# Opening pass over two tiles, outer decay levels as 32- and 64-blocks, and moved remainders at the last steps

## The reference, cut to what matters

```
x = x + 0.5 * swiglu(rmsnorm(x), w_gate, w_up, w_down)        # the opening
...
diff = bcum[..., :, None, :] - bcum[..., None, :, :]
decay = jnp.exp(jnp.where(tri, diff, -jnp.inf))
attn = jnp.einsum('zbhtk,zbhtsk->zbhts', qc, decay * kc[..., None, :, :])
...
x = x + (gelu(conv(h @ w_gate)) * (h @ w_up)) @ w_down        # the last step
gate = sigmoid(rmsnorm_2(x, norm_ple_g) @ w_ple_gate)
x = x + (p @ w_ple) * gate
return rmsnorm_2(x, final_norm_g)                             # the end
```

## Time and profile before

| | |
|---|---|
| median of 3 runs | 901.1 us (900.48 to 901.19) |
| the profiled execution | 901.16 us, its span 899.4 us |
| PE, DVE, ACT, POOL busy | 98%, 65%, 53%, 11% of the span |
| DVE remainder of a unit, L1841 / L1848 | 1259 / 1224 ns |
| ACT rounding of a unit, L1288 / L1297 | 1055 / 1058 ns |
| POOL x_lo of a chunk, L2711 | 1375 ns |
| HBM read | 155.56 MB, 174 GB/s over the span |

### The profile page before, as it was taken

The page is one execution under the profiler, slowest core; times in us unless marked ns, Lnnn a source line. Parts: engine busy times, 40 slices in busy tenths (PEclk is TensorE's granted clock), DMA queues, the critical chain, the costliest instruction groups (busy, mean ns, idle before and its releaser), DMA issues.

```text
span 899.4 us, 14824 instructions
## 1 busy us (share of the span) xinstructions
PE 877.5 (98%) x5181; PEld 733.5 (82%) x5181; DVE 587.2 (65%) x906; ACT 480.5 (53%) x727; POOL 97.3 (11%) x97
## 2 busy tenths in 40 slices
PE   6999999999999999999999999999999999999996
PEld 5788888878777778888888878878888999999875
DVE  5655555556689876655555567888776667667665
ACT  6544444447466746444444466666746445445464
POOL 6120000001000011000000022762011000000020
PEclk9999999999999999999999999999999999999998
DMA  9796666545654354755555537352246655655511
GB/s 313 228 269 197 204 212 193 174 154 165 203 175 138 95 164 140 230 191 187 186 188 186 189 105 245 119 179 101 91 147 211 206 183 179 193 186 181 190 51 47
DMA packets 122026, 157.23 MB, mean 175 GB/s; under 512 B 10047, under 2 KB 83011, under 8 KB 121984
## 3 DMA queue, kind: packets, MB, share of 16 engines
q1 hardware_dynamic: 119648, 151.65, 52.2%
q0 software_dynamic: 1888, 4.42, 2.0%
q10 hardware_dynamic: 448, 0.59, 0.2%
HBM read 155.56 MB, written 1.07 MB: 174 GB/s over the span
## 4 chain that ended last, share of the span: by engine, by line
PE 90%; DVE 5%; ACT 3%; issue 1%; DMA 1%; SPq 0%; DVEq 0%; ACTq 0%
PE bank L507 23%; PE bank L509 23%; PE bank L508 23%; PE bank L540 4%; PE bank L539 4%; PE bank L538 4%; PE bank L621 1%; DVE w_lo L1841 1%; PE bank L776 1%; PE bank L988 1%; PE bank L964 1%; DMA w_raw<-in_w_ffn_up 1%; PE bank L976 1%; ACT w_hi L1288 1%; DVE w_lo L1848 1%
## 5 line engine op out<-in xcount | busy, mean ns | idle before, releaser
L1848 DVE TENSOR_TENSOR w_lo<-w_raw,w_hi 128x1024 fp32r<-128x1024 f32 x180 | 220.2, 1224 | 176.0 <-ACT w_hi L1297 176.0
L1297 ACT ACTIVATE w_hi<-w_raw 128x1024 fp32r<-128x1024 f32 x180 | 190.3, 1058 | 207.0 <-PE bank L509 172.3
L507 PE MATMUL bank<-w_hi,x_hi 128*128 128x512 f32 (+1 forms) x688 | 276.4, 402 | 5.0 <-DVE w_lo L1841 1.8
L509 PE MATMUL bank<-w_hi,x_lo 128*128 128x512 f32 (+1 forms) x688 | 268.3, 390 | 0.0
L508 PE MATMUL bank<-w_lo,x_hi 128*128 128x512 f32 (+1 forms) x688 | 267.5, 389 | 0.0
L507 PEld LDWEIGHTS bank<-w_hi,x_hi 128*128 128x128 f32 x688 | 129.9, 189 | 35.6 <-issue 8.5
L509 PEld LDWEIGHTS bank<-w_hi,x_lo 128*128 128x128 f32 x688 | 129.7, 189 | 27.7
L1841 DVE TENSOR_TENSOR w_lo<-w_raw,w_hi 128x1024 fp32r<-128x1024 f32 x98 | 121.4, 1259 | 43.4 <-ACT w_hi L1288 43.2
L508 PEld LDWEIGHTS bank<-w_lo,x_hi 128*128 128x128 f32 x688 | 130.2, 189 | 23.9
L1288 ACT ACTIVATE w_hi<-w_raw 128x1024 fp32r<-128x1024 f32 x100 | 103.4, 1055 | 41.1 <-PE bank L509 33.6
L507 PE MATMUL bank<-w_hi,h_hi 128*128 128x512 f32 x272 | 107.6, 395 | 1.1 <-DVE h_lo L1958 0.5
(11 more groups left out here) (299 smaller groups left out, 815.0 us busy)
## 6 DMA issues: line engine op xcount, KB each, us to landing
w_raw<-in_w_ffn_gate SPq DMA_DIRECT2D x132, 256.0 KB, 2.9
w_raw<-in_w_ffn_up SPq DMA_DIRECT2D x132, 256.0 KB, 3.1
w_raw<-in_w_ffn_down SPq DMA_DIRECT2D x132, 256.0 KB, 3.0
w_raw<-in_w_in SPq DMA_DIRECT2D x104, 256.0 KB, 3.0
w_raw<-in_w_out SPq DMA_DIRECT2D x32, 256.0 KB, 3.4
w_raw<-in_w_ple_gate SPq DMA_DIRECT2D x16, 256.0 KB, 3.3
arena<-bias_rows POOLq DMA_DIRECT2D x8, 256.0 KB, 4.4
w_raw<-in_cmp_w_k SPq DMA_DIRECT2D x8, 256.0 KB, 3.7
```

The source lines that it names most:

```text
L507: pe.matmul(out_, hi, wh, start=start, stop=False)
L509: return pe.matmul(out_, lo, wh, start=False, stop=stop)
L1297: act.activation(whi[:, slot * UNIT:(slot + 1) * UNIT], raw[:, slot * UNIT:(slot + 1) * UNIT], ACT.Copy).then_inc(sem("hi_done"), 1)
L1848: dve.tensor_tensor(wlo[:, s_], raw[:, s_], whi[:, s_].bitcast(F32), ALU.subtract).then_inc(sem("lo_done"), 1)
```

## The change

- Opening, SP: x chunk 0, then the weight units 0 and 1, then x chunks 1 and 3, then the rest. ACT loads chunk 2 and four of the row loads, POOL the other seven.
- Opening, PE: nine matmuls on zeros before the first transposes, seven after the first two chunks, which are now 0 and 2 (`X_ORDER`), one of each tile. `opening()` takes the place of `tile_passes`: unit 0 over tile 0 and 1, unit 1 over both, then units 2 and 3 over tile 0, units 2 and 3 over tile 1, with the transposes of the third and fourth chunk behind the first and third of these products.
- Opening, ACT and DVE: squares of x before the rounding of unit 2, the root before that of unit 4; unit 5 after the silu of tile 0.
- Levels 6 and 7: blocks of h x h, 32 and 64, four and two for each 128 rows, each in its own strip; DVE's masked copy becomes two, one for each head of the pair, with the block's columns read repeatedly.
- Last step: convolution weights before the two scaled halves, the remainder of the second embedding unit behind the product of the convolution, that of gate unit 1 behind the second update of x, of gate unit 2 behind the fourth.
- End: the gain is multiplied ahead for chunks 0, 1 and 2; DVE multiplies the factor for chunk 0 and ACT for chunks 1 and 2; chunk 3 stays as it was. ACT stores chunk 2.

```diff
 def tile_passes / opening (PE)
+            def opening():
+                for m, j in ((0, 0), (1, 0), (0, 1), (1, 1), (0, 2), (0, 3), (1, 2), (1, 3)):
+                    if j % 2 == 0:
+                        pe.wait_ge(sem("xlo_done"), 2 * (j // 2) + m + 1)
+                    if m == 0:
+                        pe.wait_ge(*lo_ready(j + 1))
...
+                    if (m, j) == (0, 0):
+                        norm_chunk(0, 2)
+                    if (m, j) == (0, 1):
+                        norm_chunk(0, 3)
...
+            zeros = sg[:, 0:256].bitcast(BF16)
+            def warm(n):
+                for _ in range(n):
+                    pe.matmul(bank[0][:, :], zeros[:, 0:P], zeros[:, 0:512], start=True, stop=True)
+            pe.wait_ge(sem("warm_in"), 1)
+            warm(9)
...
-            for c in range(4):
+            for c in range(2):
                 norm_chunk(0, c)
+            warm(7)
             ffn(0, U_FFN1)
...
 level (PE)
-                        if 1 <= L <= 7:
-                            h, c = 1 << (L - 1), (2 * hh + blk) * P
-                            mm = pe.matmul(b[:, c:c + P], av(KMIX[pr] + hh * S + blk * P, [P]), both_ways(HQ + at, P, h),
-                                           start=True, stop=True)
+                        if L <= 7:
+                            h = 1 << (L - 1)
+                            c = (2 * hh + blk) * h
+                            for j in range(P // h):
+                                other = j ^ 1
+                                mm = pe.matmul(b[j * h:(j + 1) * h, c:c + h],
+                                               av(KMIX[pr] + hh * S + blk * P + j * h, [h]),
+                                               av(HQ + at + other * h + 1024 * (other % 2), [h]), start=True, stop=True)
...
 opening (ACT)
-            norm_hi(0, (0, 1))
+            act.dma_start(x_chunk(2), x_rows(2)).then_inc(sem("x_in2"), 16)
+            for to, r0, nr, src in row_loads[:4]:
+                act.dma_start(to[r0:r0 + nr, :], src).then_inc(sem("rows_act"), 16)
+            norm_hi(0, (0,))
             split(0)
+            norm_hi(0, (1,))
+            split(1)
...
+                squares(0, x, (m,))
+            split(2)
             norm_hi(0, (2,))
-            split(1)
+            split(3)
             norm_hi(0, (3,))
-            for v in range(2, RING):
-                split(v)
-            stats(0, x)
+            roots(0)
+            split(4)
...
 last step (DVE)
+                    if isinstance(i, int) and i > 1:
+                        conv_weights(STEPS)
+                        scaled_halves(i)
+                        return
...
-                conv_weights(STEPS)
                 conv_taps(STEPS)
...
                 conv_mul(STEPS)
+                split_step(base, STEPS - 1, 3)
...
                 split_step(base, STEPS - 1, 4)
-                split_step(base, STEPS - 1, 5)
...
-            split(U_GATE + 2)
             update = add_ffn(2, U_FFN3, 1.0)
             update(0)
             update(1)
             scaled(5, R_PLE, 0)
+            split(U_GATE + 1)
...
 end (DVE, ACT)
+            last_gain(0)
+            last_gain(2)
             gated(1, 0)
             last_mean(0)
+            last_gain(1)
             gated(1, 1)
-            dve.wait_ge(sem("gain_in"), 32)
-            last_scale(0)
+            dve.wait_ge(sem("rstd_done"), 8)
+            dve.wait_ge(sem("last_gain"), 1)
+            dve.tensor_scalar(x_chunk(0), x_chunk(0), sm(RST8), None, ALU.mult).then_inc(sem("out_ready"), 1)
             last_mean(1)
-            last_scale(1)
+            dve.wait_ge(sem("rstd_done"), 9)
+            dve.scalar_tensor_tensor(x_chunk(3), x_chunk(3), sm(RST8 + 1), gainb[:, 512:1024],
+                                     ALU.mult, ALU.mult).then_inc(sem("out_ready"), 1)
...
+            act.activation(x_chunk(1), x_chunk(1), ACT.Copy, scale=sm(RST8)).then_inc(sem("out_act"), 1)
             last_root(1)
+            act.wait_ge(sem("rstd_done"), 9)
+            act.activation(x_chunk(2), x_chunk(2), ACT.Copy, scale=sm(RST8 + 1)).then_inc(sem("out_act"), 1)
+            act.wait_ge(sem("out_act"), 2)
+            act.dma_start(out[0, P:2 * P, 0:512], x_chunk(2)).then_inc(sem("stored"), 16)
```

More of the change, by code:

```diff
@@ L428, in ffn @@
                     load_gu((base + j) % RING, wg, wu, j, slice(0, HID))
+                    if first and j == 1:
+                        x_load(1)
+                        x_load(3)
                 if first:
@@ L460, in blockload @@
                     load_cols((u + j) % RING, w, 2 * j, c0, width)
-            for c in range(2):
-                sp.dma_start(x_chunk(c), x_rows(c)).then_inc(sem(f"x_in{c}"), 16)
+            x_load(0)
             ffn(U_FFN1, t["w_ffn1_gate"][0], t["w_ffn1_up"][0], t["w_ffn1_down"][0], first=True)
@@ L622, in turn @@
                 mm.then_inc(sem("t_full"), 1)
+            def opening():
[4 more added lines that the diff above has]
+                        pe.wait_ge(*lo_ready(j + 1))
+                    wh = whi[:, j * UNIT:(j + 1) * UNIT].rearrange("p (k n) -> p k n", k=2)
+                    wl = wlo[:, j * UNIT:(j + 1) * UNIT].rearrange("p (k n) -> p k n", k=2)
+                    for kk in range(2):
+                        k = 2 * j + kk
+                        last = three(bank[m][:, :], xT(xhi, k, m), xT(xlo, k, m), wh[:, kk, :], wl[:, kk, :],
+                                     k == 0, k == 7)
+                    if m == 1:
+                        last.then_inc(sem("w_used"), 1)
+                    elif j == 3:
+                        last.then_inc(sem("tile0_full"), 1)
+                    if (m, j) == (0, 0):
+                        norm_chunk(0, 2)
+                    if (m, j) == (0, 1):
+                        norm_chunk(0, 3)
             def ffn(f, base):
@@ L671, in ffn @@
                     pe.wait_ge(sem("h_done"), 2 * n0)
-                tile_passes(base, (0, 1), ready=(0, 8)[f], nrm=(None, 2)[f])
                 if f == 0:
+                    opening()
                     columns()
+                else:
+                    tile_passes(base, (0, 1), ready=8, nrm=2)
                 gate_up_first(bias_rows if f == 0 else None)
@@ L1863, in norm_x, with means @@
                 scaled(n, gain, 3)
-            def rstd(n):
+            def means(n):
                 dve.wait_ge(sem("ss_done"), 2 * n + 2)
@@ L1870, in rstd @@
                 dve.reciprocal(sm(MS, 2), sm(MS, 2)).then_inc(sem("ms_done"), 1)
+            def rstd(n):
+                means(n)
                 dve.wait_ge(sem("rstd_done"), n + 1)
@@ L1897, in ffn @@
                 halves(0, (0,))
+                if f == 0:
+                    split(5)
                 split(base + RING)
@@ L1968, in step @@
                     split_step(base, i, 2)
+                    if isinstance(i, int) and i > 1:
+                        conv_weights(STEPS)
+                        scaled_halves(i)
+                        return
                     scaled_halves(i)
-                    for j in range(3, 4 if isinstance(i, int) and i > 1 else 6):
+                    for j in range(3, 6):
                         split_step(base, i, j)
@@ L2026, in _ @@
             dve.wait_ge(sem("gain0_done"), 1)
-            for c in range(3):
+            for c in range(2):
                 scaled(0, R_GAIN, c)
             split(0)
+            split(1)
+            scaled(0, R_GAIN, 2)
+            means(0)
+            split(2)
             scaled(0, R_GAIN, 3)
-            for v in range(1, RING):
-                split(v)
+            split(3)
+            split(4)
             def columns():
@@ L2664, in _ @@
             scaled(5, R_PLE, 2)
-            split(U_GATE + 3)
+            split(U_GATE + 2)
             scaled(5, R_PLE, 3)
-            for j in (4, 5):
+            for j in (3, 4, 5):
                 split(U_GATE + j)
```

62 lines of the change are left out of this document (39 added, 23 removed).

## The result

| | before | after |
|---|---|---|
| median of 5 runs each | 901.19 us (900.48 to 901.72) | 896.26 us (895.74 to 896.60) |
| ratio, 95% interval | | 0.9947 [0.9936, 0.9958] |
| profiled execution | 901.16, span 899.4 | 895.74, span 893.9 |
| PE busy | 877.5 | 877.1 |

A forecast was written before the change was run, and what follows sets the result against it. PE was taken to bound the kernel, busy 877.5 of 899.4 us. Opening 2.2, levels 0.4, last step 2.0 and end 0.9 sum to 5.5 us: 901.16 - 5.5 = 895.7 us, range 893.3 to 898.6.

The forecast's parts named there:

- First matmul at 10.0: Opening: with two transfers of 256 KB less ahead, the first f32r matmul starts 1.3 us earlier, bounds 0.5 and 2.0.
- The clock held: Opening: dummies keep PE at 2.4 GHz from the first matmul, saving 2.4 us, less 1.0 for transposes inside the pass.
- rival A: Opening: dummies do not hold the clock up, so it gives 0 to 0.9 us; total taken as 897.5; chance 0.20.
- End of the pass at 22.1, bias row at 28.8: Opening: pass ends 2.7 us earlier, but DVE's remainders and column copies hold the bias-row matmul until 28.8.
- Opening: 2.2 forecast: The whole opening was to give 2.2 us, bounds 0 (low clock) and 3.3.
- Levels 0.4: Levels 6 and 7: PE alone wins 1.7 us, 0.4 arrives, the rest becomes PE waiting for DVE; bounds -0.3 and 1.7.
- rival C: Level 7: 64-blocks don't run side by side and take 3.4 us instead of 1.7; total 896.9; chance 0.07.
- Rival B: Opening and levels: DVE does not pace them, giving 2.7 instead of 2.2 and 1.7 instead of 0.4; 893.9; chance 0.14.
- Last step 2.0: Third feed-forward block's last step: two PE gaps, 0.90 and 1.08 us, are covered; gain 2.0 us, bounds 1.0 and 2.1.
- The cover of 0.4 us for h_lo: Last step: the moved remainder stands ahead of h_lo, ready about 856.5 and needed at 856.95, leaving 0.4 us.
- End 0.9: After the last matmul: scaling split between DVE and ScalarE ends 1.3 us earlier; gain 0.9 us, bounds 0.3 and 1.3.
- that of the stores: End: the last two stores start together and share the rings, which costs 0.3 to 0.4 us.

The follow-up runs named there:

- the first set: The first five runs of the changed kernel, measured against the kernel before: 896.26 us against 901.19.
- level-7: The changed kernel with level 7 as one 128-wide matmul and one whole-bank copy, level 6 staying in 32-wide blocks: 895.55 us (0.9941).
- turn experiments: The changed kernel with column copies earlier, the turn of head 0 between the last unit's two tiles, ScalarE's scores ahead of its rounding: 895.20 us (0.9939).
- the second: Five more runs of the unchanged changed kernel, on one chip with three reordered kernels: 896.59 us (0.9954 to the kernel before).
- the old order: The kernel before with only the nine and seven dummy matmuls added, its order of the pass kept: 900.75 us (0.9995).

## Why the prediction was right, point by point

**First matmul at 10.0.** It was 10.34 in the first profiled execution and 9.48 to 10.60 over the seven: 0.94 us earlier where 1.3 was credited, and the clock less the transposes gave 1.61 where 1.4 was. The size of the gain from fewer transfers ahead was right within the spread of when transfers land, a spread for which the forecast had no term.

**The clock held: half right.** The spacing of 0.23 us from the start was seen in five of seven executions. In two rival A happened, for a cause that the forecast didn't name. It set rival A against the length of the dummies; the level fell behind the longest of the pauses that a late x chunk leaves between them (1.64 and 1.79 us). That goes with the pause in every trace, but no run set the pause on purpose. And A was priced at 1.8 us (897.5 against 895.7) by dummies that stay slow to the end and a low level far into the pass. It costs 0.95, for with the slow dummies running the level is back by 11.8. Why the median is 0.5 over the forecast (896.26) is another matter: the first set most likely has no fall in it.

**End of the pass at 22.1, bias row at 28.8.** Seen: 22.05 and 28.99. That DVE's remainders and copies end last was right in kind and in size; moving the copies showed that the wait stood ahead of the bias-row matmul (0.45 us). Opening: 2.2 forecast, 2.03 in the trace, 1.98 by the runs of the opening alone.

**Levels 0.4.** PE's own gain was 1.81 us against 1.7, the 64-blocks side by side as estimated: 32 records in 1.08 us, where rival C wanted 3.4. The forecast took level 7 at 1.70 us like level 6; it was 1.88, which is the difference. At the turn 0.56 arrived. Two terms were too large: the copies of level 6 were put at 0.2 and cost 0.05 (a pair of 256 columns takes 0.78 us, where 0.74 + 0.1 was taken), and the signalling was put at 0.1 and is 0.06. Behind the turn 0.17 is lost again, for which the forecast had no term. That the 0.39 left matches the forecast of 0.4 is luck in part. Rival B, DVE not the pace, fell by the level-7 and the turn experiments.

**Last step 2.0.** Measured 2.13 in the trace (the two gaps counted at 0.90 and 1.08, and 0.15 of restarting) and 1.75 by the runs of it alone. The cover of 0.4 us for h_lo held: no gap.

**End 0.9.** Measured 0.6. The chunks were ready 1.3 us sooner, as worked out (2.25 us of scaling against 3.56). The term that was too small is that of the stores, 0.3 to 0.4 forecast against 3.25 - 2.47 = 0.78: I took it as two transfers sharing the rings, but the two move in 1.5 us as before; what is lost is the overlap of the 0.9 us from a ready chunk to its first data with the second scaling.

**The sum.** By the profiled executions the parts are 2.03 + 0.39 + 2.13 + 0.6 = 5.15 us against 5.5 forecast, and 0.34 that belongs to no edit, together the 5.5 of the spans. By the medians it is 4.9 in the first set and 4.2 in the second. Signs and order of the parts were right. That the profiled execution came to 895.74 where 895.7 was forecast is luck to those 0.34 us; the medians, 0.6 and 0.9 us over it (896.26 and 896.59), are the fairer measure.

## What to carry to other kernels

When PE is the bound and gains are made by moving work to where PE stood still, ask of each gain which engine is late next, and take the answer in microseconds of slack: here DVE took 0.5 us of the opening and 1.25 of the levels' 1.81, and a later reordering of PE's work only moved the wait. A cheaper form of matmul in a stage that VectorE paces is worth the slack and no more: level 6 gave 0.56 us until the 0.67 of slack were used up, level 7 gave nothing. Dividing the scaling of the last chunks between two engines gave only what made the first of the last two stores ready sooner. Dummy matmuls that warm the clock need the useful work to follow at once and in an order that the other engines can keep up with, and where a late transfer left a pause of 1.6 to 1.8 us among them, the level fell and the execution took 1 us more.

## What the hardware showed that was not expected

- **The clock falls in the opening by a late transfer.** After nine dummies and four transposes PE stood for the next x chunk. With 0.70, 0.90, 1.15, 1.36 and 1.39 us of standing the matmuls behind were at the 2.4 GHz level (seven dummies in 1.67 us); with 1.64 and 1.79 the four transposes still took 0.66 us and the seven behind them 2.92 and 2.98, most of them at the 1.2 GHz level. In these two and in the one with nine dummies alone (1.76) the granted clock falls to 0.50 only when PE is working again, 0.5 to 0.8 us after the pause, at 8.2, 8.4 and 8.05. In the old order two pauses of 0.89 and 0.87 left it up. What else differed between these executions is not known.
- **The rise is not at a fixed time.** Without dummies the spacing fell to 0.23 us behind 13.70, some 3.4 us after the first f32r matmul; in the earlier trace rows it took 5.2 us. In three more executions with the old opening it took 2.7 (levels alone), 2.7 (end alone) and 6.1 us (last step alone), and their bias-row matmuls stand at 30.50, 30.50 and 31.57, where the earlier trace rows has 31.02. So the opening of the kernel before varies by 1.1 us as well, and its gain is better read from the eleven runs (1.98) than from one trace.
- **32-wide records in four column strips start 12 ns apart** (64 in 0.76 us), 64-wide in two strips 34 ns apart (32 in 1.08 us to the next group), 128-wide 106 to 117 ns (16 in 1.70 to 1.88 us).
- **A store's tail.** From a chunk ready to its first data it took 0.9 us (896.22 to 897.1; 890.62 to 891.5), 512 KB then moved in 1.5 us at 350 GB/s, and 0.8 to 0.9 us passed from the last data to the end of the span.
